# S5 stage of a two-block network kernel: the last block's scan inputs computed before the y ahead of it, modulation blocks dealt out 6, 8, 8, 8, 8, 8, 2, and the way back of y 6 on SP

## What is computed

```python
# S5 mixer: 64 groups of 16 channels, 64 complex states each
bu = einsum('blgh,gph->blgp', u, bb)                  # scan inputs
s  = associative_scan(s[l] = a * s[l-1] + bu[l])      # complex
y  = einsum('blgp,ghp->blgh', s_re, c_re) - einsum('blgp,ghp->blgh', s_im, c_im) + u * d_skip
y  = gelu(y);  v = y @ w_glu + b_glu
y  = v[:, :1024] * sigmoid(v[:, 1024:])
...
# second block, per layer l
mod   = silu(c) @ w_ada[l] + b_ada[l]                 # 6 * 1024 values
mod_c = silu(c_ctx) @ w_ada[l] + b_ada[l]
```

## Time and profile before

| what | us |
|---|---|
| median of 3 runs | 2878.06 (2877.31 to 2886.95) |
| the profiled execution | 2879.68 |
| its span, first to last instruction | 2877.9 |
| PE busy | 2780.8 (97%) |
| DVE busy | 1516.4 (53%) |
| POOL busy | 1304.2 (45%) |
| ACT busy | 1084.4 (38%) |

### The profile page before, as it was taken

The page is one execution under the profiler, slowest core; times in us unless marked ns, Lnnn a source line. Parts: engine busy times, 40 slices in busy tenths (PEclk is TensorE's granted clock), DMA queues, the critical chain, the costliest instruction groups (busy, mean ns, idle before and its releaser), DMA issues.

```text
span 2877.9 us, 41299 instructions
## 1 busy us (share of the span) xinstructions
PE 2780.8 (97%) x15766; PEld 2286.9 (79%) x15766; DVE 1516.4 (53%) x1961; ACT 1084.4 (38%) x1666; POOL 1304.2 (45%) x752
## 2 busy tenths in 40 slices
PE   7998987999999999999999999999999999999998
PEld 7975745878888878877788888888887778888887
DVE  7866686453324255268865432423455887452535
ACT  4435223433323233245543422322343554342433
POOL 3434323535435174388843332232347894354443
PEclk9999988999999999999999999999999999999999
DMA  5246296323323244432221221212233223233332
GB/s 188 94 164 254 93 322 200 110 81 111 95 87 102 90 125 131 145 101 91 67 88 59 81 65 59 65 60 66 67 95 117 89 66 96 73 102 95 95 102 73
DMA packets 109735, 306.88 MB, mean 107 GB/s; under 512 B 29008, under 2 KB 37328, under 8 KB 109072
## 3 DMA queue, kind: packets, MB, share of 16 engines
q1 hardware_dynamic: 87728, 284.95, 31.0%
q10 hardware_dynamic: 19504, 16.19, 1.9%
q0 software_dynamic: 2352, 3.67, 0.4%
HBM read 294.95 MB, written 7.45 MB: 105 GB/s over the span
## 4 chain that ended last, share of the span: by engine, by line
PE 87%; DVE 4%; issue 2%; POOL 2%; DVEq 1%; ACT 1%; DMA 1%; SPq 0%; ACTq 0%; POOLq 0%
PE ps L296 41%; PE ps L330 17%; PE ps L321 6%; PE ps L1963 3%; PE ps L1959 3%; PE ps L1964 3%; PE ps L1967 3%; PE ps L2376 2%; POOL wlo L257 2%; PE ps L2036 1%; PE ps L2017 1%; PE ps L749 1%; PE ps L2005 1%; DVE nacc L443 1%; PE ps L2007 1%
## 5 line engine op out<-in xcount | busy, mean ns | idle before, releaser
L257 POOL TENSOR_TENSOR wlo<-wraw,whi 128x1024 fp32r<-128x1024 f32 x373 | 924.7, 2489 | 1275.1 <-ACT whi L249 1272.7
L249 ACT ACTIVATE whi<-wraw 128x1024 fp32r<-128x1024 f32 x373 | 391.9, 1055 | 455.0 <-PE ps L296 169.9
L296 PE MATMUL ps<-xah,whi 128*128 128x512 f32 x992 | 387.9, 391 | 1.7 <-issue 1.7
L296 PE MATMUL ps<-xal,whi 128*128 128x512 f32 x992 | 387.4, 391 | 0.0
L296 PE MATMUL ps<-xah,wlo 128*128 128x512 f32 x992 | 280.1, 391 | 0.0
L2262 DVE SCALAR_TENSOR_TENSOR co<-ub,vec,co 128x512 f32<-128x512 f32 (+1 forms) x216 | 254.2, 1216 | 4.7 <-issue 0.7
L296 PEld LDWEIGHTS ps<-xah,whi 128*128 128x128 f32 x992 | 186.0, 188 | 42.8 <-issue 2.7
L296 PEld LDWEIGHTS ps<-xal,whi 128*128 128x128 f32 x992 | 186.1, 188 | 40.3
L296 PEld LDWEIGHTS ps<-xah,wlo 128*128 128x128 f32 x992 | 186.1, 188 | 40.2
L2363 POOL TENSOR_TENSOR co<-co,ct 128x512 f32<-128x512 f32 (+1 forms) x144 | 165.6, 1150 | 20.5
L296 PE MATMUL ps<-hhi,whi 128*128 128x512 f32 x408 | 159.3, 390 | 0.0
(11 more groups left out here) (418 smaller groups left out, 6003.6 us busy)
## 6 DMA issues: line engine op xcount, KB each, us to landing
wraw<-stream SPq DMA_DIRECT2D x425, 512.0 KB, 3.5
wada<-w_ada SPq DMA_DIRECT2D x96, 512.0 KB, 7.1
biasb<-attn_bias ACTq DMA_DIRECT2D x32, 256.0 KB, 3.4
xin<-x0T SPq DMA_DIRECT2D x4, 528.0 KB, 6.8
s_u<-uk ACTq DMA_DIRECT2D x8, 264.0 KB, 3.8
res<-x0T ACTq DMA_DIRECT2D x1, 2048.0 KB, 14.2
outT<-res SPq DMA_DIRECT2D x4, 512.0 KB, 2.6
s_y<-yk POOLq DMA_DIRECT2D x56, 32.0 KB, 5.2
```

What stands on the lines that cost most here:

```text
L249: act.activation(whi[:, s], wraw[:, s], ACT.Copy).then_inc(hi_done[s], 1)
L257: pool.tensor_tensor(wlo[:, s], wraw[:, s], whi[:, s].bitcast(F32), ALU.subtract).then_inc(lo_done[s], 1)
L296: last = pe.matmul(ps[:, bank, 0:b - a], w[:, s, kt], x[:, kt, c0 + a:c0 + b], start=start, stop=stop)
```

## The change

1. `ADA_S5` becomes 6, 8, 8, 8, 8, 8, 2. The groups now end with the first two blocks of rounds 2, 4 and 6 (`ADA_END` names these rounds).
2. In PE's program the turn stands behind y of rounds 2, 4 and 6. In ACT's, `ada_rows` stands at the head of the round, ahead of the wait for y, and `ada_cols` behind the gelu.
3. In round 6 PE computes w of block 7 ahead of y of block 6. DVE's write of `spv` for block 7 gets a wait for y of block 6, since `spv` has one buffer.
4. The splits of GLU units 0 and 1 on ACT move from behind the gelu and `hhi` of round 6 to ahead of that gelu.
5. `s5_y_back` of block 6 moves from POOL to SP. SP loads the first GLU weights one round later in its program, behind the two blocks of round 6.

```diff
--- before.py
+++ after.py
@@ -61,7 +61,7 @@
 N_B1 = U_FF + 4 * 16
 N_ADA = 2 * 48
 ADA_SSD = 48
-ADA_S5 = [8, 8, 8, 8, 8, 8, 0]
+ADA_S5 = [6, 8, 8, 8, 8, 8, 2]
 ADA_AT = [ADA_SSD + sum(ADA_S5[:i]) for i in range(8)]
 assert ADA_AT[7] == N_ADA
 RA = 8
@@ -776,7 +776,7 @@
             ins = pe.matmul(ps[:, turned_bank(a), 8 * j:8 * j + 8], ar[:, j * P:(j + 1) * P], pick, start=True, stop=True)
         ins.then_inc(f_c.sem, 1)
 
-    ADA_END = {1: 3, 3: 4, 5: 5}
+    ADA_END = {2: 3, 4: 4, 6: 5}
 
     def ada_dve(dve):
         dve.wait_ge(f_r.sem, f_r.past("ada", N_ADA // 16 - 1))
@@ -1389,6 +1389,8 @@
         dve.tensor_tensor(ta, sv[:, :, :, 1:], e[0], ALU.mult)
         dve.tensor_tensor(tb, sv[:, :, :, 1:], e[1], ALU.mult)
         dve.drain()
+        if i == NT - 1:
+            dve.wait_ge(f_y.sem, f_y.past("y", i - 1))
         dve.tensor_tensor(spv[:, 0], ta[:, 0], tb[:, 1], ALU.subtract)
         dve.tensor_tensor(spv[:, 1], tb[:, 0], ta[:, 1], ALU.add).then_inc(f_v.sem, 1)
         dve.drain()
@@ -1415,7 +1417,7 @@
     def s5_bat_pe(pe, i):
 
         pe.wait_ge(f_tab.sem, f_tab.past("tab", i))
-        pe.wait_ge(f_r.sem, f_r.past("ada", max([a for k, a in ADA_END.items() if k <= i - 3], default=2)))
+        pe.wait_ge(f_r.sem, f_r.past("ada", max([a for k, a in ADA_END.items() if k <= i - 2], default=2)))
         for r in range(2):
             for p in range(4):
                 last = pe.transpose(ps[:, head_bank(i) + r, p * P:(p + 1) * P], ba[:, r, p].rearrange("p k h -> p (k h)"), ident)
@@ -1490,12 +1492,14 @@
                 if i + 1 < NT:
                     ada_pe(pe, min(ADA_AT[i] + b, ADA_AT[i + 1]), min(ADA_AT[i] + e, ADA_AT[i + 1]))
 
-            if i - 1 in ADA_END:
+            more(0, 2)
+            if i == NT - 2:
+                s5_w_pe(pe, i + 1)
+            s5_y_pe(pe, i, lambda: more(2, 4))
+            if i in ADA_END:
                 pe.wait_ge(f_a.sem, f_a.past("bat", i + 1))
-                ada_turn(pe, ADA_END[i - 1])
-            more(0, 2)
-            s5_y_pe(pe, i, lambda: more(2, 4))
-            if i + 1 < NT:
+                ada_turn(pe, ADA_END[i])
+            if i < NT - 2:
                 s5_w_pe(pe, i + 1)
             more(4, 6)
             if i + 2 < NT:
@@ -1558,26 +1562,26 @@
         for i in range(NT):
             if i == NT - 1:
                 split_hi(act, U_GLU + 2)
-            if i - 1 in ADA_END:
-                ada_cols(act, ADA_END[i - 1])
+            if i in ADA_END:
+                ada_rows(act, ADA_END[i])
+            if i == NT - 2:
+                for g in range(U_GLU, U_GLU + 2):
+                    split_hi(act, g)
             act.wait_ge(f_y.sem, f_y.past("y", i))
             if i >= 2:
                 act.wait_ge(s_yw[i % 2], 128 * (i // 2))
             act.activation(yk[:, i % 2].rearrange("p (q g) c -> p g q c", g=2),
                            ps[:, 6:8, 0:4 * (NBW - 1)].rearrange("p g (q c) -> p g q c", q=4), ACT.Gelu).then_inc(f_g.sem, 1)
+            if i in ADA_END:
+                ada_cols(act, ADA_END[i])
             if i + 2 < NT:
                 s5_bat_act(act, i + 2)
                 s5_kernel_act(act, i + 2)
-                if i in ADA_END:
-                    ada_rows(act, ADA_END[i])
                 s5_move(act, i + 2)
             elif i == NT - 1:
                 split_hi(act, U_GLU + R - 1)
             if i:
                 s5_hi(act, i - 1)
-            if i == NT - 2:
-                for g in range(U_GLU, U_GLU + 2):
-                    split_hi(act, g)
         s5_hi(act, NT - 1)
 
     sgl = at("sgl", [P, 2, SEQ], SA + 16 * K)
@@ -2856,8 +2860,9 @@
                     s5_load(sp, i + 2)
                 for j in range(4, n):
                     load_ada(ADA_AT[i] + j)
-                if i == NT - 3:
+                if i == NT - 2:
                     segment(U_GLU, U_GLU, R)
+            s5_y_back(sp, NT - 2)
             s5_y_out(sp, NT - 1)
             s5_y_back(sp, NT - 1)
             segment(U_GLU + R, U_GLU + R, N_B1 - U_GLU - R)
@@ -3018,7 +3023,8 @@
             pool_units(pool, U_OUT1, 1)
             for i in range(NT - 1):
                 s5_y_out(pool, i)
-                s5_y_back(pool, i)
+                if i < NT - 2:
+                    s5_y_back(pool, i)
             for g in range(U_GLU, U_GLU + R):
                 split_lo(pool, g)
             pool_units(pool, U_GLU, (N_B1 - U_GLU) // R - 1)
```

## The result

| | before | changed |
|---|---|---|
| median of 20 runs each | 2883.47 us (2875.56 to 2893.9) | 2891.89 us (2886.21 to 2900.3) |
| the profiled execution | 2879.68 us, span 2877.9 | 2898.36 us, span 2896.6 |

The ratio is 1.0037, with a 95% interval of 1.0028 to 1.0047: 10.7 us slower, between 8 and 13.6. The two medians by themselves lie 8.4 us apart. The forecast was 6.05 slower with bounds of 2 to 10, and 2884.1 us in a range of 2879 to 2889. The sign and the size class (under 0.5%) came as forecast; the time is 7.8 us above the forecast and 2.9 above the range. The larger part of the 7.8 is the base: the three runs known before had a median of 2878.06, the twenty have 2883.47, 5.4 more.

What follows compares the result with a forecast made beforehand. PE bounds nearly the whole span (97%), but in the S5 stage the chain runs mostly through DVE. Terms 4.6 + 1.6 - 0.5 - 0.25 + 0.6 = +6.05 on 2878.06 gave 2884.1 us, range 2879 to 2889.

Steps and rivals of the forecast that it cites:

- What bounds the stage: S5 stage: the chain of waits runs mostly through DVE, whose own round is 14.87 us, longer where `cab` waits for y.
- The wait for `ada_rows` behind the moves: Rounds 2 and 4: PE idles over 6 us between y's parts, since ACT's `ar` copies come behind eight moves and `hhi`.
- +1.5: Round 2: y ends at 410.9, so DVE's `cab` starts at 410.95 instead of 409.45, 1.5 us later.
- +3.1: Round 4: y done at 444.6, so DVE's `cab` starts at 444.64 instead of 441.58, 3.1 us later.
- +1.6: Rounds 2 and 4: w of the next block comes late behind y and the turn; 1.6 us slower, bounds 0 to 3.2.
- -0.5: Round 5: PE's 2.98 us idle in w may fall elsewhere, so block 7's `bat` gains 0.5 us, bounds -1.2 to 0.
- Part 2: Round 6, w of block 7 ahead of y of block 6: scan 7 2.9 us earlier, `spv` wait free.
- Part 3: End of stage: gelu at K + 10.2 to 10.8, POOL's `wlo` at K + 15.3 instead of K + 15.5; -0.25 us.
- +0.6: GLU start: PE waits in pieces between first `wlo` products, then perhaps 3 us at low clock; 0.6 us slower, bounds 0 to 2.
- (a): Rival: `ar` copies are hidden ahead of the gelu, DVE's waits vanish; -7.8 us, 2870.3 us; chance 0.06.
- (b): Rival: low clock stays, k of blocks 4 and 6 late, DVE's tables wait; up to 16 us slower, 2894; chance 0.06.
- (c): Rival: POOL's `wlo` meets scan 7, DVE's two-input SBUF operations stand still; +15 us, 2893; chance 0.03.

Runs made afterwards that it cites:

- Experiment 3: The change with ACT's four copies of `ar` moved ahead of the eight moves of the round before; ratio to before 0.9980 (0.9967 to 0.9993).
- experiment 1: Rounds 0 to 5 of the change, with the end of the stage as before; ratio to before 1.0054 (1.0035 to 1.0074).
- Experiment 5: The change with constant matmuls on PE ahead of its waits for the second, third and fourth `wlo`; ratio to before 1.0024 (1.0007 to 1.0041).
- experiment 4: Before, with only `s5_y_back` of block 6 moved from POOL to SP; ratio to before 1.0013 (0.9999 to 1.0028).
- experiment 6: Experiment 3 with DVE's scan 7 ahead of `hlo` of block 4 and ACT's round 6 gelu ahead of the splits; ratio to before 0.9996.
- experiment 7: Experiment 6 with SP also issuing the eight DMAs of `yk` of block 6; ratio to before 0.9983 (0.9968 to 0.9997).
- experiment 9: Experiment 7 with 3 and 2 constant matmuls at PE's two remaining waits for `wlo`; ratio to before 0.9972 (0.9954 to 0.9989).
- experiment 8: Experiment 4 plus a POOL wait: first `wlo` not before scan 7 is done; ratio to before 1.0007 (0.9990 to 1.0024).

## Why the prediction was right and wrong

- **What bounds the stage**: right. The loss in the middle runs over DVE's wait for y, and DVE's rounds 3 and 5, without a wait, stayed at 14.88 us.
- **The wait for `ada_rows` behind the moves**: right in mechanism, place and releaser. The idle was forecast at over 6 us and was 7.24 and 6.95. Experiment 3 shows the cause by moving that one call.
- **"+1.5" for round 2 was mis-sized**: +3.54. The step that failed is taking `ka` and the moves from the trace of before. `ka` of block 3 came 6.56 us behind scan 2 instead of 5.21, since PE, which now had less to do, idled 1.97 us ahead of `bat` and did k at the low clock; and from `ka` to `hhi` it took 6.1 us instead of 5.5. These two make about the missing 2.0. **"+3.1" for round 4** was +2.27: there `ka` came 1.36 us earlier, the moves took 0.95 us longer, and the clock came back within y. Together 5.8 against 4.6, above my upper bound. One execution is a thin base for these sizes: by the means over executions above, the two waits grew by 6.9.
- **"+1.6" for the late w**: right in size, 1.61 in round 2 and 0 in round 4. I had called it the middle between 0 and 3.2, and it was one round at each end, as in experiments 1 and 5. Fills took it away, so it is the low clock's, as said.
- **"-0.5" for block 7's `bat`**: +0.1. A PE idle without a releaser fell into round 5 again (1.59 us). Experiments 1 and 5, with the same rounds, have 4.60 and 4.59 us from scan 6 to K instead of 6.00, so the term depends on where that idle falls.
- **Part 2**: right. Scan 7 started 2.5 us earlier against K and y of block 7 ended 2.5 us earlier (2.9 forecast for both); the wait at `spv` cost nothing.
- **Part 3**: the gelu was forecast at K + 10.2 and was at K + 10.7, `wlo` at K + 15.3 and was at K + 15.8. So "-0.25" was +0.28. The shape was right: what the move to SP gives, the later gelu takes.
- **The low clock at the end, "+0.6", was mis-sized most**: from the fourth `wlo` to the first L296 product it is 17.63 us before and 20.41 after, **+2.78**, above my bound of 2. The mechanism was named, the three waits came as forecast, but the step that failed is the price: I took some 3 us at the low clock, as a case that might not come. The rows show 6.8 us at 0.50, with PE busy nearly all of the time from the fourth `wlo` on. Experiment 5 shows the cause by keeping PE busy through the waits.
- **The base**: a median of three runs, 5.4 us below that of twenty. Of the 7.8 us between forecast and measured time it is the larger part; the other 2.4 are the terms (8.4 between the medians against 6.05). With the right base the measured time would lie in the range; with the right terms alone it would still be half a us above it. The bounds +2 to +10 hold the 9.6 of the profile and the 8.4 of the medians, not the 10.7 of the ratio, and that is luck in part: three terms were beyond their own upper bounds (5.8 against 4.6, 2.78 against 2, +0.1 against 0), and the late w, 1.6 against 3.2, made up for them.
- **The rivals**: (a) fell, since nothing passed ACT's moves. (b) was not seen: DVE's tables never waited for k in rounds 3 or 5 (such a wait does occur, 1.13 us in round 1 of before, and the sum had no term for it). (c) did not happen here, but did in experiments 1 and 4; the prediction had its margin of 3 us right, and a neighbouring order loses it. It also had the Trainium skill's rule ("SBUF — State Buffer", section "SBUF: two separate sides") on its side: one engine keeps the other out. By experiment 4 the trace agrees in that, with one difference: DVE's row starts 0.11 us ahead of POOL's, and it was DVE that stood still, over three `wlo` and not over one. The prediction took its own row to agree with "whoever starts first", but that row reads like experiment 4: `hlo` starts at 479.76, 0.25 us ahead of `wlo` (480.01), and it is `hlo` that is stretched.

## What to carry to other kernels

When work is dealt out anew so that a wait leaves the critical engine, look at what stands in front of the releasing instruction in its own engine's program: four copies of 2.4 us in all came behind eight DMA issues and one more copy, and 2.6 us of idle became 7. Price an idle of TensorE with the slower work behind it, at full. And when POOL starts earlier, check which VectorE operations on two inputs in SBUF it will meet; the price was anything from one POOL operation to the whole run of them. A base from three runs was 5.4 us off here, over half of the effect.

## What the runs showed that was not expected

- One DVE `tensor_tensor` stretched from 0.69 to 7.60 us (experiment 4) and 7.40 us (experiment 1) beside POOL `tensor_tensor` that followed each other without a gap, and its result was what PE waited for.
- Adding 3.9 us of useless matmuls made the end 2.2 us shorter (experiment 5).
- Eight DMA issues on ACT took from 5.2 to 6.3 us; with them ahead of the copies, such a difference moves y with it (0.95 us in round 4).
- In experiments 6, 7 and 9 PE waited four or five times for the modulation's weights (`DMA wada<-w_ada`, 0.17 to 1.10 us each), in experiments 3, 4 and 8 once or twice; the profiles of before and of the change show no such wait. What these waits cost is not measured.
- Executions whose programs are the same up to scan 1 reach it between 376.14 and 386.99 us. That is as much as the effect in question; only the stretches of the trace, and many runs, tell it apart.
